# Second expert mixture: token rows sorted through memory, and the hidden products in two column halves

## The reference, cut to what matters

```python
def hier_moe(x2d, ...):                      # x2d: (T, 1024)
    ...                                      # router: one group of 4, then two of its 4 experts
    def expert_step(acc, p):
        w1e, w3e, w2e, c = p                 # (1024,512), (1024,512), (512,1024), weight per token
        h = jax.nn.silu(x2d @ w1e) * (x2d @ w3e)
        return acc + c[:, None] * (h @ w2e), None
    ...

for l in range(DEPTH):
    m = conformer_conv(...) if l == 0 else diff_attention(...)
    h = layernorm(ALPHA * h + m, ...)
    f = hier_moe(h, ...)
    h = layernorm(ALPHA * h + f, ...)
return h[:, N_META:]
```

## Time and profile before

| | |
|---|---|
| median of 3 runs | 806.4 us (806.14 to 809.16) |
| the profiled execution's own time | 805.26 us |
| its span | 803.2 us |
| TensorE busy | 692.0 us (86%) |
| VectorE / ScalarE / GpSimd busy | 300.6 / 218.1 / 30.4 us |
| mean granted TensorE clock | 0.938 |
| DMA | 174.55 MB, 217 GB/s over the span |
| second mixture | weights asked for from 607.4 us, last product of an item at 776.7 us; 21 items, 7 experts |

### The profile page before, as it was taken

How to read it: one execution, slowest core, us unless ns; L and a number is a source line. 1 busy time by engine, 2 the same in 40 slices (tenths; PEclk the granted TensorE clock), 3 DMA queues, 4 the chain that set the end, 5 groups by cost and what they waited for, 6 DMA issues and landing times.

```text
span 803.2 us, 19040 instructions
## 1 busy us (share of the span) xinstructions
PE 692.0 (86%) x7553; PEld 444.3 (55%) x7554; DVE 300.6 (37%) x896; ACT 218.1 (27%) x564; POOL 30.4 (4%) x46
## 2 busy tenths in 40 slices
PE   5999889889989899895569999959976999998863
PEld 4887658545545455452158457847852555554431
DVE  0799731461222212120344107871163222222215
ACT  1541350331212222120331014554050222222230
POOL 0000000200000000000200001100020000000001
PEclk9999999979999999997769999999988999999986
DMA  9999024206799699997499100020007986917904
GB/s 301 365 392 364 12 105 158 105 1 218 277 406 383 247 405 368 355 346 275 137 390 387 43 0 2 1 105 1 1 8 298 399 319 232 403 49 287 362 30 158
DMA packets 86825, 174.55 MB, mean 217 GB/s; under 512 B 7784, under 2 KB 21969, under 8 KB 86785
## 3 DMA queue, kind: packets, MB, share of 16 engines
q1 hardware_dynamic: 72912, 157.36, 52.9%
q10 hardware_dynamic: 11601, 8.13, 3.3%
q0 software_dynamic: 2272, 8.52, 2.9%
HBM read 162.99 MB, written 11.01 MB: 217 GB/s over the span
## 4 chain that ended last, share of the span: by engine, by line
PE 68%; DMA 14%; DVE 8%; ACT 4%; issue 4%; POOL 2%; SPq 0%; POOLq 0%; DVEq 0%; ACTq 0%
PE ps L681 17%; DMA ring<-in_moe_w 11%; PE ps L702 8%; PE ps L503 8%; PE ps L600 4%; PE ps L572 4%; PE ps L583 4%; PE ps L791 3%; PE ps L810 3%; PE ps L653 3%; PE ps L738 2%; PE ps L664 2%; PE ps L537 1%; DVE work L1398 1%; PE ps L522 1%
## 5 line engine op out<-in xcount | busy, mean ns | idle before, releaser
L681 PE MATMUL ps<-ring,work 128*32 128x256 f32 x2816 | 171.8, 398 | 28.5 <-DMA ring<-in_moe_w 14.7
L681 PEld LDWEIGHTS ps<-ring,work 128*32 128x32 f32 x2816 | 99.5, 114 | 93.2 <-issue 41.5
L900 ACT ACTIVATE work<-ps 128x256 f32<-128x256 f32 (+4 forms) x160 | 55.5, 363 | 226.2 <-PE ps L702 95.6
L1398 DVE TENSOR_TENSOR work<-work,ps 64x256 f32<-64x256 f32 x44 | 18.7, 424 | 219.7 <-ACT work L1000 219.7
L702 PE MATMUL ps<-ring,work 128*32 128x256 f32 x1408 | 89.8, 384 | 0.4 <-DMA ring<-in_moe_w 0.4
L1181 DVE SCALAR_TENSOR_TENSOR work<-work,wdw 128x272 f32<-128x272 f32 x150 | 65.1, 499 | 1.0
L653 PE MATMUL ps<-tok,work 128*32 128x256 f32 x928 | 64.3, 385 | 0.0
L503 PE MATMUL ps<-xT,ring 128*128 128x272 f32 x256 | 61.3, 403 | 0.3 <-DVE xT L1158 0.3
L702 PEld LDWEIGHTS ps<-ring,work 128*32 128x32 f32 x1408 | 38.9, 109 | 33.4 <-DVE work L1400 10.4
L503 PEld LDWEIGHTS ps<-xT,ring 128*128 128x128 f32 x256 | 50.0, 196 | 11.0 <-DVE xT L1158 0.4
L1000 ACT ACTIVATE work<-ps 64x256 f32<-64x256 f32 x44 | 16.5, 375 | 129.0 <-PE ps L681 129.0
(11 more groups left out here) (225 smaller groups left out, 738.4 us busy)
## 6 DMA issues: line engine op xcount, KB each, us to landing
ring<-in_moe_w SPq DMA_DIRECT2D x120, 1024.0 KB, 11.9
ring<-in_conv_w_pw SPq DMA_DIRECT2D x12, 1024.0 KB, 11.8
ybuf<-work ACTq DMA_DIRECT2D x44, 128.0 KB
ybuf<-const POOLq DMA_DIRECT2D x2, 2048.0 KB, 8.1
ring<-in_kv_w_k SPq DMA_DIRECT2D x4, 1024.0 KB, 9.2
ring<-in_kv_w_v SPq DMA_DIRECT2D x4, 1024.0 KB, 10.8
ring<-in_attn_w_q SPq DMA_DIRECT2D x4, 1024.0 KB, 11.4
ring<-in_attn_w_o SPq DMA_DIRECT2D x4, 1024.0 KB, 10.8
```

What stands on the lines that cost most here:

```text
L681: last = pe.matmul(ps[SLOTS * q:SLOTS * (q + 1), 0, 0:256], xTg[:, k, :], w[:, k, (q % 2) * 256:(q % 2 + 1) * 256], start=(k == 0), stop=( ...
L900: return act.activation(dst, src, ACT.Copy)
```

## The change

For layer 1 only, the gather by one-hot product inside the items goes. Instead GpSimd writes the token rows to memory in slot order once (`xsort`, four indirect DMAs of 128 rows of 4 KB), and for each further item ScalarE loads 128 KB of it into `xg`. Item 0 is still gathered by `pick`. The products with `w1` and `w3` are made in two column halves, to PSUM banks 0 and 5, with Silu, gate, transpose and copy for each half, and the product with `w2` is split around the second transpose. `xsort` is filled with finite numbers at the start by a transfer of 36·32 rows of 4 KB. Some semaphores are merged (`in_taps` into `in_vec`, `in_router` and `in_lam` into `in_layers`). Below, `sorted_item` is TensorE's, the first `sorted_items` ScalarE's, the second VectorE's.

```diff
+            pool.dma_start(xsort.rearrange("(a p) d -> p a d", p=P),
+                           const[:, 0:D].unsqueeze(1).broadcast_to([P, SORTED * SLOTS // P, D])).then_inc(sem("y_filled0"), 16)
+            def sort_rows():
+                pool.wait_ge(sem("y_filled0"), 32)
+                pool.wait_ge(sem("pos_ready"), 2)
+                pool.wait_ge(sem("tok_ready1"), 2 * TILES[1])
+                for j in range(TILES[1]):
+                    for c in range(2):
+                        pool.indirect_dma_start(
+                            out=xsort, out_offset=bass.IndirectOffsetOnAxis(ap=pos_i[:, 1, c * 3 + j:c * 3 + j + 1], axis=0),
+                            in_=tok[:, j, :], in_offset=None,
+                        ).then_inc(sem("xsort_ready"), 16)
...
                 scale(l)
+                if l == 1:
+                    sort_rows()
                 pool.wait_ge(sem("tab_ready"), l + 1)
...
+            def sorted_item(g, b, it):
+                def hidden(part):
+                    for k in range(NC_):
+                        if k % 4 == 0 and part == 0:
+                            for m in range(2):
+                                pe.wait_ge(*arrived(b + m, k // 4, it))
+                        for q in range(QUARTERS):
+                            at = (q % 2) * 256 + part * P
+                            last = pe.matmul(ps[SLOTS * q:SLOTS * (q + 1), HIDDEN_BANK[part], 0:P], xTg[:, k, :],
+                                             w[q // 2][:, k, at:at + P], start=(k == 0), stop=(k == NC_ - 1),
+                                             skip_group_check=True)
+                    return last
+                def turn_hidden(part):
+                    pe.wait_ge(sem("hs_ready1"), g * 2 + (part + 1))
+                    pe.sem_inc(sem("turn_begun"), 1)
+                    pe.transpose(ps[:, 4, part * 64:(part + 1) * 64], hs[64:128, part * P:(part + 1) * P],
+                                 ident[64:128, 64:128]).then_inc(sem("h_turned1"), 1)
...
+                pe.wait_ge(sem("xT_ready1"), g + 1)
+                hidden(0).then_inc(sem("h_begun1"), 1)
+                hidden(1).then_inc(sem("h_ready1"), 1)
+                turn_hidden(0)
+                pe.wait_ge(sem("xg_loaded"), g * 16 + 16)
+                for m in range(2):
+                    last = pe.transpose(ps[:, 3, m * P:(m + 1) * P], xg[:, m * P:(m + 1) * P], ident)
+                last.then_inc(sem("xg_turned1"), 1)
+                pe.wait_ge(sem("hT_ready1"), g * 2 + 1)
+                pe.wait_ge(*arrived(b + 2, 0, it))
+                output(0, True, False)
+                turn_hidden(1)
+                pe.wait_ge(*arrived(b + 2, 1, it))
+                output(2, False, False)
+                pe.wait_ge(sem("hT_ready1"), g * 2 + 2)
+                output(1, False, False)
+                output(3, False, True).then_inc(sem("y_ready1"), 1)
...
+            def sorted_items(n):
+                def load(g):
+                    act.wait_ge(sem("xg_turned1"), g)
+                    act.dma_start(xg, xsort[bass.ds(g * SLOTS, SLOTS), :].rearrange("s (q c) -> q s c", q=QUARTERS)).then_inc(sem("xg_loaded"), 16)
+                act.wait_ge(sem("xsort_ready"), 16 * 2 * TILES[1])
+                load(1)
+                def item(g, buf, turn):
+                    act.wait_ge(sem("h_begun1"), g + 1)
+                    act.activation(hs[64:128, 0:P], ps[0:64, HIDDEN_BANK[0], 0:P], ACT.Silu).then_inc(sem("silu_ready1"), 1)
+                    act.wait_ge(sem("h_ready1"), g + 2)
+                    act.activation(hs[64:128, P:2 * P], ps[0:64, HIDDEN_BANK[1], 0:P], ACT.Silu).then_inc(sem("silu_ready1"), 1)
+                    load(g + 2)
+                    act.wait_ge(sem("y_ready1"), g + 2)
...
+            def sorted_items(n):
+                with dve.Fori(0, n) as g:
+                    gate(g, 0)
+                    move_hidden(g, 0)
+                    gate(g, 1)
+                    move_gathered(1, g + 1, True)
+                    move_hidden(g, 1)
```

More of the change, by code:

```diff
@@ L53 @@
 MIN_ITEMS = 2 * SEQ // SLOTS
+SORTED = MAX_ITEMS + 4
 TILES = [(T0 + P - 1) // P, SEQ // P]
@@ L162, in trunk @@
         ybuf = [nc.dram_tensor(f"ybuf{l}", (MAX_ITEMS * SLOTS, D), F32, kind="Internal").ap() for l in range(2)]
+        xsort = nc.dram_tensor("xsort", (SORTED * SLOTS, D), F32, kind="Internal").ap()
         def cst(name):
@@ L704, in item, with output @@
                 last.then_inc(sem(f"y_ready{l}"), 1)
+            def sorted_item(g, b, it):
+                w = [brick(b + m).rearrange("p (k n) -> p k n", k=NC_) for m in range(2)]
+                w2 = brick(b + 2).rearrange("p (k n) -> p k n", k=4)
+                def hidden(part):
[14 more added lines that the diff above has]
+                                 ident[64:128, 64:128]).then_inc(sem("h_turned1"), 1)
+                def output(k, first, final):
+                    for q in range(QUARTERS):
+                        last = pe.matmul(ps[SLOTS * q:SLOTS * (q + 1), 1, 0:256], hT[:, k, :], w2[:, k, q * 256:(q + 1) * 256],
+                                         start=first, stop=final, skip_group_check=True)
+                    return last
+                pe.wait_ge(sem("xT_ready1"), g + 1)
[15 more added lines that the diff above has]
+                output(3, False, True).then_inc(sem("y_ready1"), 1)
@@ L718, in expert @@
                         with pe.Fori(lo, hi) as g:
-                            item(l, g, b, it)
+                            if l == 0:
+                                item(l, g, b, it)
+                            else:
+                                sorted_item(g, b, it)
                 with pe.Fori(0, 5) as it:
@@ L986, in post @@
                 act.activation(e2[:, 0:n], e2[:, 0:n], ACT.Exp).then_inc(sem("e2_ready"), 1)
+            def sorted_items(n):
[11 more added lines that the diff above has]
+                    act.wait_ge(sem("y_ready1"), g + 2)
+                    act.wait_ge(sem(f"y_stored1_{buf}"), turn * 16 + 16)
+                    move(ysb[:, buf, :], ps[:, 1, 0:256]).then_inc(sem("y_moved1"), 1)
+                    act.wait_ge(sem("y_moved1"), g + 1)
+                    act.dma_start(ybuf[1][bass.ds(g * SLOTS, SLOTS), :].rearrange("s (q c) -> q s c", q=QUARTERS),
+                                  ysb[:, buf, :]).then_inc(sem(f"y_stored1_{buf}"), 16)
+                with act.Fori(0, n >> 1) as turn:
+                    item(turn * 2, 0, turn)
+                    item(turn * 2 + 1, 1, turn)
+                with act.If(n & 1):
+                    item(n - 1, 0, n >> 1)
+                act.wait_ge(sem("xg_loaded"), n * 16 + 16)
+                combine(1, 0)
             def mixture(l):
@@ L1378, in pick_item @@
                                             pos2[:, c, 0:n].unsqueeze(2).broadcast_to([P, n, SLOTS]), ALU.is_equal)
+                if l == 1:
+                    step(ins)
+                    dve.tensor_tensor(pick[:, 0:n, :], eq[:, 0], eq[:, 1], ALU.add).then_inc(sem("pick_ready1"), 1)
+                    return
                 ins.then_inc(sem(f"peq_ready{l}"), 1)
@@ L1389, in move_gathered, with gate, move_hidden @@
                                 ps[:, 3, 0:256].rearrange("p (m q s) -> p m q s", m=2, q=QUARTERS)).then_inc(sem(f"xT_ready{l}"), 1)
+            def sorted_items(n):
+                def gate(g, part):
+                    dve.wait_ge(sem("silu_ready1"), g * 2 + (part + 1))
+                    h = hs[64:128, part * P:(part + 1) * P]
+                    dve.tensor_tensor(h, h, ps[64:128, HIDDEN_BANK[part], 0:P], ALU.mult).then_inc(sem("hs_ready1"), 1)
+                def move_hidden(g, part):
+                    dve.wait_ge(sem("h_turned1"), g * 2 + (part + 1))
+                    dve.tensor_copy(hT.rearrange("p (a m) s -> p m a s", a=2)[:, part],
+                                    ps[:, 4, part * 64:(part + 1) * 64].rearrange("p (a s) -> p a s", a=2)).then_inc(sem("hT_ready1"), 1)
+                with dve.Fori(0, n) as g:
[4 more added lines that the diff above has]
+                    move_hidden(g, 1)
             def mixture(l):
```

31 lines of the change are left out of this document (17 added, 14 removed).

## The result

The changed kernel takes 852.96 us (median; 848.22 to 855.29), the one before on the same chip 806.27: a ratio of 1.0573, 95% interval [1.0533, 1.0612]. I had forecast 802.0 in a range of 794 to 830, so sign and range are wrong. The profiled execution spans 853.4 us against 803.2, 50.2 more.

A forecast was written before the change was run, and what follows sets the result against it. TensorE's chain was taken to bound the second mixture's items, with the row load as the new wait. Terms −13.5 (shorter periods), +3.4 (loaded periods) and +5.8 (start) sum to −4.3 us; forecast 802, range 794 to 830.

The forecast's parts named there:

- Hidden products, 3.55 an item: TensorE's products with w1 and w3 in column halves take 3.55 us an item, range 3.45 to 3.97.
- rival 4: Halves don't pipeline, each group of four waits for its loads: hidden products 6.9 us, about 873 us; chance 0.04.
- Between hidden products and output, 2.94: TensorE's remaining item time: drain 0.14, half transpose 0.25, row transposes 0.44, output 1.86, interruption 0.25; sum 2.94 us.
- Period 6.49: An item of the second mixture with all loads hidden takes 3.55+2.94 = 6.49 us, against 7.165 before.
- so I stay with these: 5.8 to 6.9: The row load beside streaming weights lands in 5.8 to 6.9 us, as earlier loads on ScalarE's queue did.
- landing + 0.75: Loop from row transposes through the next load's issue and landing to the next transposes: landing plus 0.75 us.
- It also queues behind the item's own store: Row load waits behind the store on ScalarE's queue: 6.5 to 7.0 us a period, 6.75 taken in loaded stretches.
- Rival 1: Row load as slow as a store: landing 8.4, loaded period 9.15, 12 such periods cost 32, 830 us; chance 0.22.
- The start, +5.8: Until item 0 ends: sort delays weights 5.2, second column half +1.2, rest of item 0 gains 0.6; +5.8 us.
- At nothing: Parts priced at zero: the 4.7 MB fill of xsort, merged semaphores, one-hot work leaving VectorE, the last row loads.
- Gain of 13.5 with all hidden: 20 periods of the second mixture each 0.675 us shorter if the row load is hidden: 13.5 us gained.
- Rival 3: Row load hidden (fits in 5.7 us) and weights come before the sort: 793.5 us; chance 0.10.

The follow-up runs named there:

- no_stores: The changed kernel with the items' output stores in the second mixture left out, so part of the computation is missing: 847.08 us, 1.051 of the kernel before.
- no_sort: The changed kernel without the four indirect writes of token rows in slot order, so part of the computation is missing: 846.98 us, 1.0498 of the kernel before.
- wide_rows: The changed kernel with each 128 KB row load as 32 pieces of 4 KB and eight transposes of 32 rows: 823.34 us, 1.0196 of the kernel before.
- order_two: order_fixed with two staging buffers, rows loaded two items ahead and copied by ScalarE: 806.67 us, 1.0014 of the kernel before.
- order_fixed: The changed kernel with row loads in memory order, VectorE's copy putting the slots back in order: 809.48 us, 1.004 of the kernel before.

## Why the prediction was wrong, step by step

- *Hidden products, 3.55 an item*: right, 3.49 in quiet items (up to 4.14 at a lowered clock). That is 27 ns for each load and product; the 81 ns that the Trainium skill, TensorE: Matmul & The Clock Gate, section Back-to-back issue gap, gives for such a pair did not hold in column tiles of 32, and rival 4 fell. (Four tiles run together, so by an estimate from the 27 ns each tile has a pair every 109 ns.)
- *Between hidden products and output, 2.94*: right; the quiet periods of 6.46 and 6.29 leave 2.97 and 2.80. Period 6.49 stands, if 0.1 too high.
- *The row load, "so I stay with these: 5.8 to 6.9"*: this step failed. Measured are 9.09 to 11.33. The loads of the earlier trace rows were taken as nearest for being loads of up to 128 pieces. But in the trace of the kernel before, each of those five loads ends with 16 packets of 4 bytes, and the store of the earlier trace rows with four. The store was nearer, as it has the same outermost size, and thus the same four engines. The upper bound of 8.4 was too low too: the load of no_stores, with nothing else on its queue, takes 9.7 to 12.1 beside the weights. The rule "landing + 0.75" held: 10.04 + 0.75 is 10.79, measured 10.78.
- *It also queues behind the item's own store*: refuted as a cause by no_stores.
- *Rival 1* had the mechanism (as slow as a store) and the count of 12 loaded periods. Its price was mis-sized: 12·(10.78−6.49) = 51.5 instead of 32. With −13.5 for 20 shorter periods, +7.1 for the three at the edges, −0.5 for the quiet ones and −4.0 for two jumps that now lie in waits, the loop is 40.6 longer, as measured.
- *The start, +5.8*: measured +8.6. The sort is 7.2 of it (no_sort). Part of that is the delay of the weights, as I had it: the second part of item 0's products starts at 628.1 instead of 623.1 in no_sort. The rest stands in a row: sort landed (10.93), then the first row load (11.23). "Both fall before item 0's hidden products end" held for the sort (landed at 624.4, products over at 632.5) and not for the load (landed at 635.6), by the landing again: in wide_rows, whose load lands in 5.2 us, the first turn comes at 631.5, straight behind the products.
- *At nothing*: the 4.7 MB fill landed in 19.3 us and the second mixture begins 0.9 us later; right.
- *Gain of 13.5 with all hidden*: the sum left out what is late next. Order_two has all hidden, and its 20 periods take 145.2 us instead of 147.3: 20·6.4 is 128, and most of the rest are the wait for the last expert's weights (a period of 14.62) and the stops put down to "issue" (7.5 us ahead of the hidden products, 3.6 before). Rival 3, 793.5, is not reached with the load hidden: order_two's first turn comes 4.0 us later than before the change, and without these 4.0 it would take some 803 (an estimate from its 806.7).

The landing explains most of the miss, and not all. With a landing of 5.9, inside the forecast's 5.8 to 6.9, order_fixed takes 809.5 and not 802.0: 43.5 of the 51.0 us between forecast and measurement are the landing, and the other 7.5 are the gain of the halves, which does not arrive. So a load as fast as forecast would have made the number nearly right and the change still no gain.

## What to carry to other kernels

Before pricing a transfer from another one, compare the order of dimensions, not only bytes and pieces: an outermost size of 4 puts it on 4 of 16 DMA engines, and on ScalarE's queue the packets of 4 bytes at its end count them (GpSimd's load has 16 of them with 3.3 engines busy). A shorter item pays only until the next stream (here the last expert's weights) or a stop for its longer code ends last. Test a new small transfer first without its neighbours, then in another shape.
